# When the norms and splits of x, the maxima, the exponentials and the queries are issued: a schedule shifted by slots in a one-core decoder step

## The reference

```
xn = rmsnorm(x, g_mix);  q, k, v, u, h, gb, gc = split(xn @ w_in)        # 2048 -> 5120
att  = dilated sliding-window attention (16 heads of 64; windows/dilations (128,1),(512,4),(2048,16))
       prompt: over its own 256 keys;  decode: over 2048 cached keys and 8 new ones per batch
ssm  = S5 scan over u (32 groups, 64 complex states), gelu, GLU;   conv = gb * conv3(gc * h)
x    = x + concat(rmsnorm(att), rmsnorm(ssm), rmsnorm(conv)) @ w_out
x    = x + (silu(rmsnorm(x) @ w_gate) * (rmsnorm(x) @ w_up)) @ w_down;   y = rmsnorm(x, g_final)
```

## Time and profile before

| | us |
|---|---|
| median of 3 runs (1516.5 to 1517.22) | 1516.99 |
| the profiled execution | 1517.05 |
| its span, first to last instruction | 1515.0 |

### The profile page before, as it was taken

The page is one execution under the profiler, slowest core; times in us unless marked ns, Lnnn a source line. Parts: engine busy times, 40 slices in busy tenths (PEclk is TensorE's granted clock), DMA queues, the critical chain, the costliest instruction groups (busy, mean ns, idle before and its releaser), DMA issues.

```text
span 1515.0 us, 28035 instructions
## 1 busy us (share of the span) xinstructions
PE 1487.5 (98%) x11367; PEld 1421.2 (94%) x11367; DVE 840.8 (56%) x1061; ACT 633.4 (42%) x1027; POOL 224.4 (15%) x317
## 2 busy tenths in 40 slices
PE   9989999999999999999999999999999999999997
PEld 9989877888877999999999999999999999999997
DVE  7779789983477677445444444445444433343334
ACT  6444545557666354433333333333333333234332
POOL 7874335310540000000000000000000000000100
PEclk9999999999999999999999999999999999999999
DMA  7536799999888444444444444444444444444442
GB/s 268 166 124 232 273 349 357 363 385 388 296 332 307 154 142 151 153 146 147 151 152 146 146 151 152 148 145 150 152 149 145 150 153 152 145 150 153 147 151 106
DMA packets 93271, 296.40 MB, mean 196 GB/s; under 512 B 9728, under 2 KB 11008, under 8 KB 92800
## 3 DMA queue, kind: packets, MB, share of 16 engines
q1 hardware_dynamic: 92608, 294.10, 56.9%
q10 hardware_dynamic: 576, 1.08, 0.2%
HBM read 289.06 MB, written 5.43 MB: 194 GB/s over the span
## 4 chain that ended last, share of the span: by engine, by line
PE 84%; DVE 8%; ACT 3%; POOL 2%; issue 2%; DMA 0%; DVEq 0%; ACTq 0%
PE ps L2147 20%; PE ps L2148 20%; PE ps L2146 20%; PE ps L1990 5%; PE ps L2030 2%; PE ps L1992 2%; PE ps L2036 2%; PE ps L2031 2%; PE ps L1835 2%; DVE wlo L1112 2%; PE ps L1841 2%; PE ps L2099 1%; PE ps L2098 1%; PE ps L2097 1%; ACT whi L716 1%
## 5 line engine op out<-in xcount | busy, mean ns | idle before, releaser
L1465 DVE TENSOR_TENSOR wlo<-raw,whi 128x1024 fp32r<-128x1024 f32 x264 | 325.2, 1232 | 519.9 <-ACT whi L989 519.8
L989 ACT ACTIVATE whi<-raw 128x1024 fp32r<-128x1024 f32 x264 | 279.9, 1060 | 606.2 <-PE ps L2148 601.7
L2148 PE MATMUL ps<-xh,wlo 128*128 128x320 f32 x1400 | 432.6, 309 | 0.0
L2146 PE MATMUL ps<-xh,whi 128*128 128x320 f32 x1400 | 432.6, 309 | 0.0
L2147 PE MATMUL ps<-xl,whi 128*128 128x320 f32 x1400 | 432.6, 309 | 0.0
L2147 PEld LDWEIGHTS ps<-xl,whi 128*128 128x128 f32 x1400 | 262.8, 188 | 0.0
L2148 PEld LDWEIGHTS ps<-xh,wlo 128*128 128x128 f32 x1400 | 262.8, 188 | 0.0
L2146 PEld LDWEIGHTS ps<-xh,whi 128*128 128x128 f32 x1400 | 262.8, 188 | 0.0
L2146 PE MATMUL ps<-hh,whi 128*128 128x320 f32 x696 | 215.1, 309 | 0.0
L2147 PE MATMUL ps<-hl,whi 128*128 128x320 f32 x696 | 215.1, 309 | 0.0
L2148 PE MATMUL ps<-hh,wlo 128*128 128x320 f32 x696 | 215.1, 309 | 0.0
(11 more groups left out here) (340 smaller groups left out, 1872.4 us busy)
## 6 DMA issues: line engine op xcount, KB each, us to landing
raw<-in_w_gu SPq DMA_DIRECT2D x176, 512.0 KB, 3.7
raw<-in_w_dn SPq DMA_DIRECT2D x88, 512.0 KB, 3.7
raw<-in_w_in SPq DMA_DIRECT2D x78, 512.0 KB, 5.0
kv<-in_cv SPq DMA_DIRECT2D x64, 512.0 KB, 7.2
kv<-in_ck SPq DMA_DIRECT2D x32, 768.0 KB, 6.7
kv<-in_ck SPq DMA_DIRECT2D x32, 512.0 KB, 6.9
raw<-in_w_out SPq DMA_DIRECT2D x32, 512.0 KB, 3.8
raw<-in_cv SPq DMA_DIRECT2D x16, 512.0 KB, 7.7
```

Source lines behind the costliest of these rows:

```text
L989: act.activation(whi[:, j % SPL, :], raw[:, j % RAW, :], ACT.Copy).then_inc(S["w_hi"], 1)
L1465: v.tensor_tensor(wlo[:, j % SPL, :], raw[:, j % RAW, :], whi[:, j % SPL, :].bitcast(F32), ALU.subtract) \
L2146: t_.matmul(out, whi[:, slot, w], ah[:, k, :], start=(k == 0), stop=False)
L2148: last = t_.matmul(out, wlo[:, slot, w], ah[:, k, :], start=False, stop=(k == 2 * units - 1))
```

## The change

Only the schedule changes; the operations are the same.

- `NORM_AT` gives the slots of `normed_x` and `normed_high`: 12, 13, 16, 17, 18, 19, 20, 21. `normed_low(j)` stays one slot behind, and now ahead of the `normed_x` of its slot.
- The scan's matrices: products in slot 16 and sums in 21, instead of 15 and 16; transposes and copies in slot 22 instead of 18. GpSimd no longer waits for the transposes.
- SCAN_TIME: the slots of `turn_probabilities` weigh 10.
- `maxima(b)` goes to the end of VectorE's slot +4; `spread_bias(b)` and all four exponentials to ScalarE's slot +5; `queries(b)` to slot -2.
- The scan mixer's correcting steps come in slot 76 with the reciprocal; SUM_CONV, with all that hangs on it, is 84.
- The bank that held the turned new values is released by the second of their two copies.

```diff
-BT_SLOT, VN_SLOT = 18, 56
-NORM_SLOT, PLAIN = 12, 2
+BT_MADE, BT_SUMS, BT_SLOT, VN_SLOT = 16, 21, 22, 56
+NORM_AT, PLAIN = (12, 13, 16, 17, 18, 19, 20, 21), 2
-SUM_SSM, SUM_CONV = 76, 83
+SUM_SSM, SUM_CONV = 76, 84
-        SCAN_TIME = [0 if s % U_IN == U_IN - 2 else 10 if s < SCAN1 else 12 if s < SCAN2 else 19 for s in range(SCAN_END)]
+        TURN_SLOTS = [first + TURN for first in START_OF]
+        SCAN_TIME = [0 if s % U_IN == U_IN - 2 else 10 if s in TURN_SLOTS else 10 if s < SCAN1 else 12 if s < SCAN2 else 19 for s in range(SCAN_END)]
-                    "vn": lambda: ("vn_moved", key[1] + 1),
+                    "vn": lambda: ("vn_moved", 2),
 # ScalarE
-                if NORM_SLOT <= s < NORM_SLOT + U_IN:
-                    normed_high(s - NORM_SLOT)
+                for j in range(U_IN):
+                    if NORM_AT[j] == s:
+                        normed_high(j)
-                for b in batches(s, -1):
+                for b in batches(s, -2):
                     queries(b)
...
                 for b in batches(s, 4):
                     spread_maxima(b)
+                for b in batches(s, 5):
                     spread_bias(b)
-                    exponent(b, (0, 1))
-                for b in batches(s, 5):
-                    exponent(b, (2, 3))
+                    exponent(b, range(4))
 # VectorE
                 if s + 3 >= U_IN:
                     low(s + 2)
-                if NORM_SLOT <= s < NORM_SLOT + U_IN:
-                    normed_x(s - NORM_SLOT)
-                if NORM_SLOT < s <= NORM_SLOT + U_IN:
-                    normed_low(s - NORM_SLOT - 1)
+                for j in range(U_IN):
+                    if NORM_AT[j] + 1 == s:
+                        normed_low(j)
+                for j in range(U_IN):
+                    if NORM_AT[j] == s:
+                        normed_x(j)
...
-                if s == BT_SLOT - 3:
+                if s == BT_MADE:
                     input_matrices()
-                if s == BT_SLOT - 2:
+                if s == BT_SUMS:
                     input_sums()
...
-                for b in batches(s, 4):
-                    maxima(b)
...
                 if s == SUM_SSM:
-                    scales_first(1, rstd_s)
+                    scales(1, rstd_s)
                 if s == SUM_SSM + 1:
-                    scales_rest(1, rstd_s)
                     normed(ZU, V_OUT + 12, rstd_s)
                 for i, part in scan_parts(s):
                     scan(i, part)
+                for b in batches(s, 4):
+                    maxima(b)
 # GpSimd
-            pool.wait_ge(S["bt_done"], 2)
             pool.wait_ge(S["q_zero"], 1)
```

## The result

| | before | after |
|---|---|---|
| median of 4 runs, us | 1516.74 (1516.18 to 1517.22) | 1544.15 (1543.02 to 1545.55) |
| profiled execution, us | 1517.05 | 1543.69 |
| its span, us | 1515.0 | 1541.9 |
| mean granted clock | 0.996 | 0.990 |

The change makes the kernel 1.8% slower: ratio 1.0181, 95% interval 1.0164 to 1.0199. The prediction was 1527.2 us, range 1519 to 1539. The direction and the mechanism of part 1 were right, and the size was not: of 26.9 us in the span, 10.1 were forecast. The largest of the missed terms is the edit of SCAN_TIME, which was costed at nothing and costs 5.6 us here; then come 3.6 us of relief in part 2 that did not come or were given back, 3.0 of the clock, which falls four times between 78 and 123 us instead of once, and 2.5 of part 3.

A forecast was written before the change was run, and what follows sets the result against it. TensorE, busy 98% of the span, was taken as the bound. From the 1515.0 us span, 14.4 + 3.4 - 5.7 - 1.5 - 1.3 + 0.8 gave 1525.1, with 2.05 outside it 1527.2 us; range 1519 to 1539.

The forecast's parts named there:

- part 1: Units 18 to 23: splits one slot ahead make TensorE wait on xl six times, 4.2 then about 3.0 us; +14.4 us.
- the edit of SCAN_TIME: Some thirty scan parts move one slot, mostly earlier; nothing comes of it, bounds -0.5 and +1 us.
- part 2: Slots 42 to 48: earlier queries and regrouped maxima and exponentials remove TensorE stalls and a clock fall; -2.3, -3.4 and -1.5 us.
- the clock: In the stalls before units 18 to 23: one fall to half rate, +3.4 us, bounds none and 17.
- part 3: Slots 76 to 78: the 1.7 us TensorE wait at 427.7 us goes, prompt_norms(5) comes later; -1.3 us, bounds -1.7 and +0.5.
- VectorE would be saturated: Sign for the stretch of the six stalls, between 72 and 111 us: VectorE, now saturated there, waits for whi.
- Rival (b): In the stalls before units 18 to 23 the clock falls in most: 17 instead of 3.4 us, 1541 us; chance 0.10.
- the rule of the Trainium skill: Idle gaps between matmul bursts return TensorE to half rate; most of six stalls would cost a fall, some 14 us more.
- rival (c): Later reliefs fail: four exponentials in one slot hold back transposes and weights, stalls at 186 and 214 us stay; 1534, chance 0.10.
- come 0.5 later: Slot 76: prompt_norms(5), on which TensorE waits 0.7 us, is delayed 0.5 us by the three correcting steps moved there.
- Part 4: SUM_CONV 84: the 1.6 us wait on sqc goes, but later evictions hold units; +0.8 us, bounds -1.6 and +2.

The follow-up runs named there:

- experiment 1: Kernel before with only the new NORM_AT, order of splits, scan-matrix slots 16, 21 and 22, and GpSimd's dropped wait: 1537.64 us against 1517.01, ratio 1.0135.
- experiment 4: Changed kernel with NORM_AT 12, 13, 15, 16, 17, 18, 19, 20, so six of eight splits come one slot earlier: 1529.57 us, ratio 1.0085.
- experiment 8: Kernel before with only the scan matrices moved (products slot 20, sums 21, transposes and copies 22) and without GpSimd's wait for the transposes: 1522.09 us, ratio 1.0040.
- experiment 5: Changed kernel with 11 unused filler matmuls of ones ahead of each of units 18 to 23, keeping TensorE busy while it waits: 1538.20 us, ratio 1.0144.
- experiment 3: Kernel before with the new slots for queries, bias, exponentials and maxima and the wait for the second copy, old SCAN_TIME: 1515.38 us, ratio 0.9986.
- experiment 6: Changed kernel with the SCAN_TIME list of the kernel before: 1539.08 us, ratio 1.0145.
- experiment 7: Kernel before with only the scan mixer's three correcting steps moved to slot 76: 1517.58 us, ratio 1.0006.
- experiment 11: Kernel before with new slots for queries, bias, exponentials and maxima, the second-copy wait and SUM_CONV 84, old SCAN_TIME: 1513.45 us against 1516.86, ratio 0.9979.
- Experiment 9: Kernel before with a single part of the scan, (7, 4), in slot 47 instead of 48: 1522.98 us against 1516.86, ratio 1.0043.

## Why the prediction was wrong, step by step

**Part 1, the chain: right.** Six stalls on xl: 4.2, 3.4 and 0.3, three of 3.0 and one of 2.1 us, against 4.2 and five of 2.98. Undisturbed rounds are 6.88 against 6.91. The stall before unit 18 has the size worked out, but unit 18 starts at 77.84 instead of 76.25: unit 17 ends at 73.64, not at 72.1. About half of these 1.6 us is where this profile starts (unit 17 starts 0.8 us later than before, and only 0.05 earlier in experiment 1, where unit 18 starts at 76.91). The other half is a relief that was forecast ahead of unit 17 and didn't come: the wait on L1124 shrinks from 1.4 to 0.5 us, but unit 16 waits 0.7 for its wlo instead. Two things told beside the chain were wrong. VectorE would be saturated: it is idle for 2.7 to 5.2 us of a round, and the loop is bound by its latency. And without the rounds the sums of slot 21 and the transposes at the end of unit 22 would be clear of each other by most of a unit: in experiment 4 the transposes wait 2.4 us for them, in experiment 8, with the products late too, 6.67.

**The clock: the right kind, the size too small.** The term was one fall of 6.8 us, 3.4 us, with bounds 0 and 17. There are four, each 3.4 us long, worth 5.7 us by experiment 5. From unit 18 to unit 24 the forecast has 38.3 us and the trace 44.7, which is 6.4 more; the term of 3.4 covers a part, and 3.0 are missing. Rival (b), with a fall in most stalls, was right in the number of falls, four of six, and wrong in their price, 17 us. Its 1541 lies near the 1544.15 measured by luck, since most of what the forecast missed is elsewhere. That each stall follows 3.7 us of solid matmuls, which was put against it, did not keep the clock up in four of the six; what kept it up in the other two isn't shown. By the rule of the Trainium skill cited in the prediction ("TensorE: Matmul & The Clock Gate", section "Why this matters for your kernels"), the sum would have been 14 us higher; the trace agrees with the rule in that four of six stalls here were followed by a fall, and not in that two stalls of 3.0 us were followed by none.

**SCAN_TIME: the step that failed.** "TensorE hardly waits for VectorE from 232 to 360 us, so nothing comes of it", with bounds of -0.5 and +1. It costs 5.6 us in this kernel and 8.1 alone, and one part alone, moved by one slot, costs 6.1 (medians). It moves 19 parts, not some thirty, and all of them earlier. The step looked at where VectorE is late. What moved was an order on TensorE: the slot of a part also sets the slot of the read-out, and with it who gets bank 5 first. The absence of a wait in the trace before was no evidence, since in the old order the question doesn't come up. What would have shown it: for each moved part (4i + 3, 4), the order in which its bank is filled, before and after.

**Part 2, the rest: the reliefs right, what they give back not.** -7.7 us up to unit 49 against -7.2 (2.3 + 3.4 + 1.5); without SCAN_TIME -6.2, because the wait on smax near slot 43 grows from 1.0 to 1.4 us and the fall was worth 3.0. That this wait stays, as the prediction said, is so in experiments 3 and 6; with the new SCAN_TIME it is gone. Not seen: 1.6 us at units 53 and 56, and 1.0 at unit 74, where the prompt's outputs wait for evictions behind exponentials; so -3.6 in all. In experiment 3 3.3 us more are lost at unit 86. That more exponentials in one slot hold back the transposes was weighed for slot 47 only; rival (c) named the mechanism for the two old stalls, and it came in new places.

**Part 3: wrong in sign.** -1.3 forecast, +1.2 measured (experiment 7: +1.35 in the profile, +0.8 by the medians), beyond its bound of +0.5. The step that failed is "come 0.5 later": they come 1.7 later, since the idle time it counted on lies ahead of the moved work in the same queue, and the clock falls behind the longer stall, which the term had at nothing.

**Part 4: right.** +0.8 forecast, +1.2 measured. Without it, though, part 2 costs 3.3 us in the same place, so with part 2 in the kernel part 4 is worth -2.2 from unit 83 on (experiment 11 against 3).

The errors add up: 1.6 and 3.0 up to unit 24, 5.6 for SCAN_TIME, 3.6 for the rest of part 2, 2.5 for part 3 and 0.4 for part 4 are 16.7, and the span is 16.8 over the forecast (26.9 less 10.1). The parts measured alone add up too, by their medians and within the noise: 20.6 for part 1, 8.1 for SCAN_TIME, -3.4 for the rest of part 2 with part 4 (experiment 11) and 0.8 for part 3 are 26.1 us, against 27.4 for the change.

## What to carry to other kernels

When a list of weights deals work over slots, list what else is placed by the same function (here the read-outs, and with them the order in which a bank is taken) and compare the orders before and after, one resource at a time: one part of 80, moved by one slot, cost 6 us. A result needed ahead of unit u has to be issued at least two slots ahead, not one, if the slot's first work waits for the unit before; here two slots still cost 7.5 us up to unit 24 against the three of before. Idle time can take up moved work only when it lies behind that work in the same queue. And when a program's runs differ by 2 us, compare the profiled one with their median before its microseconds are shared out.

## What was not expected of the hardware

The length of a stall alone doesn't say whether TensorE's clock falls. The wait of 1.99 us for bmat ahead of the transposes is the same in the kernel before and in experiment 11, and comes 0.4 us earlier there. Before, the clock stays at 1.00; in experiment 11 it is 0.50 for 3.4 us behind it:

```profile
79.14 1.76 PE L1955 MATMUL ps<-ident,bmat 128*128 128x128 f32 x8 [1.99 <-DVE bmat L1240]
```

```profile
79.40:82.80 3.40, 3.40 (x16) 3.40 (x15) 3.15 (x5) 1.90 (x3) 3.24 (x6) 0.50 0.41 122
```

It costs nothing there: unit 21 starts 1.1 us later than before, but at unit 22 the wait for weights that was 1.57 us is 0.19. In the rounds, stalls of 3.0 to 3.4 us were followed by a fall at times and at times not: experiment 6 has 20.5 us of half clock there and the changed kernel 13.7, with the same order of work on TensorE and VectorE up to that point. Experiment 9 has both cases in one kernel: the same wait for bmat, 1.97 us and 0.2 us later than before, is followed by a fall, so its coming earlier is not what made the difference; and the stall of 2.28 us in front of unit 48 is followed by none, where that of 2.29 in the kernel before is followed by 6.8 us of half clock. What decides was not tested.
